# Per-head norm statistics kept in 16 rows, with root and reciprocal there, and spread back by matmuls

## The reference, cut to what matters

```python
# RWKV, before the scan
kk = (k * k_k).reshape(hd)                    # hd = (b, t, 16 heads, 64)
kk = kk / jnp.maximum(jnp.linalg.norm(kk, axis=-1, keepdims=True), 1e-12)
# RWKV, after the scan
mean = jnp.mean(y, axis=-1, keepdims=True)
var = jnp.mean(jnp.square(y - mean), axis=-1, keepdims=True)
y = (y - mean) * lax.rsqrt(var + RW_LNX_EPS) * lnx_w + lnx_b
y = y + jnp.sum(rh * kh * r_k, axis=-1, keepdims=True) * vh
out = (y.reshape(b, t, c) * g) @ w_o
# latent attention, rmsnorm per head
q_nope = rmsnorm(q[..., :64], qn_norm)        # 16 heads of 64
q_pe = rope(rmsnorm(q[..., 64:], qr_norm), pos)   # 16 heads of 32
k_nope = rmsnorm(einsum('...r,rhd->...hd', c, w_uk), kn_norm)
```

## Time and profile before

| | us |
|---|---|
| median of the runs (3) | 3170.84 |
| lowest, highest | 3169.41, 3178.54 |
| span of the profiled execution | 3169.1 |
| PE busy | 2695.0 (85%) |
| DVE busy | 1607.7 (51%) |
| ACT busy | 1070.8 (34%) |
| POOL busy | 174.8 (6%) |

### The profile page before, as it was taken

One profiled execution on the slowest core, in us unless ns is written; L12 is line 12 of the kernel. 1 busy time (PEld: TensorE's weight loads), 2 busy tenths in 40 slices (PEclk: granted clock), 3 DMA queues, 4 the chain that ended last, 5 costly groups with the idle time before them and its releaser, 6 DMA issues. The chain is left out here.

```text
span 3169.1 us, 48791 instructions
## 1 busy us (share of the span) xinstructions
PE 2695.0 (85%) x21151; PEld 2385.4 (75%) x21151; DVE 1607.7 (51%) x2358; ACT 1070.8 (34%) x1798; POOL 174.8 (6%) x176
## 2 busy tenths in 40 slices
PE   6939985998847899979989888978997939985999
PEld 5728854998724678869989866678997718864999
DVE  5384336644362577756434843265536374326643
ACT  4333112433311344434334620044434332203442
POOL 0020011000000000000000132200000020011000
PEclk8969867999865899989999965589998978967999
DMA  4210001444200222214434301323442210001442
GB/s 152 90 66 3 6 28 60 153 147 159 98 0 0 67 67 67 67 54 157 149 124 146 138 27 63 131 99 120 147 147 104 83 40 30 6 27 53 147 151 105
DMA packets 44133, 275.70 MB, mean 87 GB/s; under 512 B 5216, under 2 KB 5248, under 8 KB 14096
## 3 DMA queue, kind: packets, MB, share of 16 engines
q1 hardware_dynamic: 43680, 271.95, 24.1%
q0 software_dynamic: 240, 0.64, 0.1%
HBM read 256.32 MB, written 16.24 MB: 86 GB/s over the span
## 5 line engine op out<-in xcount | busy, mean ns | idle before, releaser
L315 PE MATMUL banks<-rounded,rounded 128*128 128x320 f32 x3184 | 1009.8, 317 | 165.3 <-DVE rounded L331 69.1
L316 PE MATMUL banks<-rounded,rounded 128*128 128x320 f32 x3184 | 995.7, 313 | 0.0
L317 PE MATMUL banks<-rounded,rounded 128*128 128x320 f32 x3184 | 995.2, 313 | 0.0
L305 DVE TENSOR_TENSOR rounded<-weight_ring,rounded 128x1024 fp32r<-128x1024 f32 x398 | 487.2, 1228 | 513.4 <-ACT rounded L298 513.1
L315 PEld LDWEIGHTS banks<-rounded,rounded 128*128 128x128 f32 x3184 | 609.4, 191 | 177.3 <-DVE rounded L331 74.3
L316 PEld LDWEIGHTS banks<-rounded,rounded 128*128 128x128 f32 x3184 | 609.7, 191 | 3.6
L317 PEld LDWEIGHTS banks<-rounded,rounded 128*128 128x128 f32 x3184 | 608.8, 191 | 0.0
L298 ACT ACTIVATE rounded<-weight_ring 128x1024 fp32r<-128x1024 f32 x398 | 419.2, 1058 | 414.6 <-PE banks L317 360.1
L942 PE MATMUL banks<-arena 64*64 64x64 f32 x4032 | 146.3, 225 | 22.8 <-PEq L788 20.3
L942 PEld LDWEIGHTS banks<-arena 64*64 64x64 f32 x4032 | 134.4, 140 | 31.0 <-issue 29.2
L470 ACT ACTIVATE arena<-banks 128x320 f32<-128x320 f32 x128 | 56.0, 438 | 247.9 <-PE banks L317 247.9
(11 more groups left out here) (361 smaller groups left out, 3593.1 us busy)
## 6 DMA issues: line engine op xcount, KB each, us to landing
weight_ring<-in_panels SPq DMA_DIRECT2D x206, 1024.0 KB, 4.7
arena<-in_pages SPq DMA_DIRECT2D x64, 320.0 KB, 3.4
arena<-in_ssm SPq DMA_DIRECT2D x8, 1024.0 KB, 4.8
out_ssm_sample<-arena SPq DMA_DIRECT2D x8, 1024.0 KB, 3.8
arena<-in_wkv SPq DMA_DIRECT2D x2, 2048.0 KB, 8.2
out_wkv_sample<-arena SPq DMA_DIRECT2D x2, 2048.0 KB, 6.2
consts<-in_consts SPq DMA_DIRECT2D x1, 1673.5 KB, 9.7
residual<-in_x SPq DMA_DIRECT2D x1, 1280.0 KB, 5.6
```

The costliest lines, as they stand in the source:

```text
L305: self.k.nc.vector.tensor_tensor(self.k.w_lo[:, i % SPLIT], self.raw(i), self.k.w_hi[:, i % SPLIT].bitcast(F32), ALU.subtract)\
L315: mm(out, hi, x_hi, start=start, stop=False)
L316: mm(out, hi, x_lo, start=False, stop=False)
L317: return mm(out, lo, x_hi, start=False, stop=stop)
```

## The change

Two constants are added, `pick64` and `pick32`, and two helpers. `pick(w, i)` is a window of 16 columns with which a product of a tile's squares puts the means of its heads into their rows of a 16-row result; eight (four) products add up to the statistics of all heads in one bank. `spread` copies rows back: for each head of a tile, one product of a broadcast column of the identity with the 16 rows fills the head's 64 (32) partitions of a bank. Root, clamp and reciprocal then run on 16 rows of 320 (256) columns.

- In the preparation, DVE multiplies the keys straight from the spread banks; PE's bonus products wait for these products (`kk`).
- In the output, DVE scales from the spread banks; bias, gate and remainder follow in an interleaved order on DVE; POOL has no part any more, and the third weight remainder is put in front of the reciprocal.
- In the latent projection, ACT squares rotary queries and keys tile by tile inside the loop; PE sums two tiles later (`stat`), and spreads queries (`to_rows`) within the loop from tile 22 on through three banks in turn; the key rows are spread behind the rotation's products.

```diff
+    for w, n in ((64, 30), (32, 28)):
+        add(f"pick{w}", (np.arange(n)[None] == n - 16 + p[:, None] // w) / w)
+    def pick(self, w, i):
+        c, n = CONST_COLS[f"pick{w}"]
+        first = n - 16 - P // w * i
+        return self.consts[:, c + first:c + first + 16]
+    def spread(self, out, w, i, rows):
+        c, _ = CONST_COLS["ident"]
+        for n in range(P // w):
+            h = P // w * i + n
+            ins = self.nc.tensor.matmul(out[n * w:(n + 1) * w, :], self.consts[0:16, c + h:c + h + 1].to_broadcast([16, w]), rows,
+                                        start=True, stop=True)
+        return ins
...
# preparation, DVE
-            for g in range(2):
-                vec.wait_ge(*pe_did.at("norm", 4 * g + 3))
-                v.tensor_scalar(g3(T2)[:, 4 * g:4 * g + 4, :], allbanks[:, 4 * g:4 * g + 4, :], 1e-24 / 64, None, ALU.max)\
...
-                v.reciprocal(T2[:, h], T2[:, h]).then_inc(*vec_did.tick("inv", g))
+            vec.wait_ge(*pe_did.at("norm"))
+            v.tensor_scalar(inv, k.bank(0, T)[0:16, :], 1e-24 / 64, None, ALU.max).then_inc(*vec_did.tick("clamp"))
+            vec.wait_ge(*act_did.at("root"))
+            v.reciprocal(inv, inv).then_inc(*vec_did.tick("inv"))
             for i in range(KT):
-                ins = v.scalar_tensor_tensor(T1[:, cols(i)], K[:, cols(i)], k.param(f"k_k{j}", i), T2[:, cols(i)], ALU.mult, ALU.mult)
+                vec.wait_ge(*pe_did.at("inv", i))
+                ins = v.scalar_tensor_tensor(T1[:, cols(i)], K[:, cols(i)], k.param(f"k_k{j}", i), k.bank(i, T), ALU.mult, ALU.mult)
# preparation, PE
-                nc.tensor.matmul(k.bank(i, T), k.const("mean64"), T2[:, i * T:(i + 1) * T], start=True, stop=True)\
+                ins = nc.tensor.matmul(k.bank(0, T)[0:16, :], k.pick(64, i), T2[:, i * T:(i + 1) * T], start=i == 0, stop=i == KT - 1)
+            ins.then_inc(*pe_did.tick("norm"))
+            pe.wait_ge(*vec_did.at("inv"))
+            for i in range(KT):
+                k.spread(k.bank(i, T), 64, i, inv).then_inc(*pe_did.tick("inv", i))
+            pe.wait_ge(*vec_did.at("kk"))
...
# output, DVE
+            split.lo(vec, 2)
+            vec.wait_ge(*act_did.at("root"))
+            v.reciprocal(RS, RS).then_inc(*vec_did.tick("rs"))
+            for n in range(KT + 4):
+                if n < KT:
+                    vec.wait_ge(*pe_did.at("rs", n))
+                    v.scalar_tensor_tensor(Y[:, n, :], Y[:, n, :], k.param(f"lnx_w{j}", n), k.bank(n, T), ALU.mult, ALU.mult)\
+                        .then_inc(*vec_did.tick("w", n))
...
+                if 0 <= n - 2 < KT:
+                    i = n - 2
+                    vec.wait_ge(*vec_did.at("b", i))
+                    v.tensor_tensor(Y[:, i, :], Y[:, i, :], G[:, i, :], ALU.mult).then_inc(*vec_did.tick("gated", i))
+                if 0 <= n - 4 < KT:
+                    rest_vec(k, vec, act_did, vec_did, lambda i: Y[:, i, :], yh, yl, n - 3, first=n - 4)
# latent projection, PE, in the loop over tiles n
+                if 9 <= n < 29:
+                    stat(*kinds[n - 2])
+                if 22 <= n < 26:
+                    to_rows("p", n - 22)
+                if 26 <= n < 31:
+                    to_rows("q", n - 26)
+            for i in range(5, KT):
+                to_rows("q", i)
+            pe.wait_ge(*vec_did.at("qpn", 3))
...
+            pe.wait_ge(*vec_did.at("rk"))
+            pe.wait_ge(*vec_did.at("qn", KT - 1))
+            for i in range(KT):
+                ins = k.spread(k.ps[:, 4 + i // 2, (i % 2) * TP:(i % 2 + 1) * TP], 64, i, RK)
# latent projection, ACT, in the loop: roots of 16 rows behind tiles 17, 20 and 28
+                if n == 17:
+                    act.wait_ge(*pe_did.at("stat", "qn"))
+                    s.activation(RQ, k.ps[0:16, 4, 0:T], ACT.Sqrt, bias=k.eps(0, slice(0, 16))).then_inc(*act_did.tick("rootq"))
...
# latent projection, DVE
             v.reciprocal(RQ, RQ).then_inc(*vec_did.tick("rq"))
-            v.scalar_tensor_tensor(QN, QN, gain, RQ, ALU.mult, ALU.mult).then_inc(*vec_did.tick("qn"))
+            for i in range(KT):
+                vec.wait_ge(*pe_did.at("rows", "q", i))
+                v.scalar_tensor_tensor(QN[:, i, :], QN[:, i, :], gain, k.bank((7, 4, 5)[(4 + i) % 3], T), ALU.mult, ALU.mult)\
+                    .then_inc(*vec_did.tick("qn", i))
+                if i == 5:
+                    vec.wait_ge(*act_did.at("rootk"))
+                    v.reciprocal(RK, RK).then_inc(*vec_did.tick("rk"))
```

More of the change, by code:

```diff
@@ L851, in _ @@
             ins.then_inc(*act_did.tick("factor"))
[L852 to L855, removed]
+            act.wait_ge(*vec_did.at("clamp"))
+            s.activation(inv, inv, ACT.Sqrt, scale=64.0).then_inc(*act_did.tick("root"))
             act.wait_ge(*pool_did.at("before"))
@@ L1192, in stage_rwkv_output @@
     flat = lambda a: a.rearrange("p a b -> p (a b)")
[L1193 removed]
+    SQ, RS = k.at(RW["AR"], KT, T), k.at(RW["BK"], T, rows=16)
     yh, yl = k.rounded(RW["BK"] + W, KT, T), k.rounded(RW["BK"] + 2 * W, KT, T)
@@ L1208, in _ @@
                 pe.wait_ge(*act_did.at("sq", i // 4))
-                nc.tensor.matmul(k.bank(i, T), k.const("mean64"), SQ[:, i, :], start=True, stop=True).then_inc(*pe_did.tick("var", i))
-            pe.wait_ge(*act_did.at("root", 1))
+                ins = nc.tensor.matmul(k.bank(0, T)[0:16, :], k.pick(64, i), SQ[:, i, :], start=i == 0, stop=i == KT - 1)
+            ins.then_inc(*pe_did.tick("var"))
+            pe.wait_ge(*vec_did.at("rs"))
+            for i in range(KT):
+                k.spread(k.bank(i, T), 64, i, RS).then_inc(*pe_did.tick("rs", i))
             out_project_pe(k, pe, split, yh, yl, KT, lambda e, i: e.wait_ge(*vec_did.at("xl", i)))
@@ L1219, in _ @@
             split.hi(act, 1)
-            for g, fs in halves:
-                act.wait_ge(*pe_did.at("var", 4 * g + 3))
-                nc.scalar.activation(RS[:, fs, :], allbanks[:, fs, :], ACT.Sqrt, bias=k.eps(1)).then_inc(*act_did.tick("root", g))
+            act.wait_ge(*pe_did.at("var"))
+            nc.scalar.activation(RS, k.bank(0, T)[0:16, :], ACT.Sqrt, bias=k.eps(1, slice(0, 16))).then_inc(*act_did.tick("root"))
             split.hi(act, 2)
-            round_act(k, act, act_did, pool_did, lambda i: Y[:, i, :], yh, KT, "gated")
+            round_act(k, act, act_did, vec_did, lambda i: Y[:, i, :], yh, KT, "gated")
             out_project_act(k, act, split, KT)
[L1227 to L1231, removed]
         @block.vector
@@ L1240, in _ @@
                 split.lo(vec, i)
[L1241 to L1248, removed]
+            split.lo(vec, 2)
[6 more added lines that the diff above has]
+                        .then_inc(*vec_did.tick("w", n))
+                if 0 <= n - 1 < KT:
+                    i = n - 1
                     vec.wait_ge(*vec_did.at("w", i))
```

85 lines of the change are left out of this document (41 added, 44 removed).

## The result

The changed kernel takes 3103.09 us (median of 4 runs, 3097.12 to 3114.55), the one before 3171.61 beside it: ratio 0.978, 95% interval 0.977 to 0.980. That is 68.5 us faster where 53.8 were forecast, and 0.9 us under the low end of the range. The profiled execution took 3105.45 us with a span of 3103.7, 65.4 us less than the span before.

The account below looks back on a forecast made before the run. The prediction took VectorE's reciprocals to bound the three changed stretches. Savings of 2 x 9.1 + 2 x 12.4 + 11.0 - 0.2 = 53.8 us off 3170.8 gave 3117 us, range 3104 to 3140.

Parts of the forecast that it names:

- Preparation: Two preparations: short root and reciprocal, then eight spreads at 1.07 us a bank; 9.1 us saved each.
- Output: Two outputs: short reciprocal, DVE the bound from the fourth bank at 1.83 us a bank; 12.4 us saved each.
- Latent projection: One latent projection: sums and spreads move into the tile loop, shortening the tail behind it; 11.0 us saved.
- Each inserted sum or spread pays two changes: Latent projection's loop: every inserted small matmul pays two changes of matmul shape, 0.2 us each, beside its passes.
- The part behind the loop: Latent projection after its tile loop: few full-sized matmuls there, so rotations and key spreads were priced at 1.2 GHz.
- I take the loop at 2.4 GHz and rotations and key spreads at 1.2 GHz, 5.6 more: Latent projection: lower clock only behind the loop adds 5.6 us, cutting the saving from 16.6 to 11.0 us.
- Rival 1: Clock rises during the spreads and stays up, also through the latent projection: 3107 us, chance 0.17.
- Rival 2: Clock falls in the latent loop with the first spread and stays down to the stage's end: 3138 us, chance 0.25.
- Rival 3: Column blocks of the spreads do not overlap, at 1.2 GHz, making the kernel slower: 3193 us, chance 0.03.

Follow-up runs that it names:

- gate_pool: Changed kernel with the output's gating put back on GpSimd, all else the same: 3100.54 us.
- pairs: Changed kernel with the latent projection's sums placed in pairs behind every second tile: 3098.18 us.
- latent_only: Changed kernel with the preparation and output changes taken back, so only the latent projection is changed: 3154.81 us.
- halves: Changed kernel with the spreads of preparation and output reordered, all upper 64-column matmuls first, then all lower: 3129.08 us.
- pairs_gate_rope: Changed kernel with latent sums paired, output gating on GpSimd, and the sine product ahead of the key products: 3104.61 us.

## Why the prediction was right and where it failed

- **Preparation: right, step by step.** Root, 2.14 us reciprocal at 176.28, pitch 1.07 at 0.50, end 187.87; 9.0 saved of 9.1.
- **Output: right within 1.3 us, in part by luck.** The first output tile was ready 35.0 us after the stage's start at 451.9 (forecast about 35). VectorE is the bound from the fourth tile on, as forecast, and at 1.72 us a tile in place of 1.83 its last remainder came 0.8 us earlier than forecast; but the tile then took 2.1 us more and not 1.1, as TensorE's passes at the lower clock lagged behind. The two misses cancel. gate_pool, meant to take load off VectorE, slowed its biases, and so does not show by itself how far behind TensorE is. In layer 3 the old output was 1.3 us longer than in layer 0, and so the saving there 13.7.
- **Latent projection: the failed step.** "Each inserted sum or spread pays two changes", at 0.2 each. Between the copies of the first and the last tile this made 25.5 us of additions (the 26.4 of the prediction less one spread, which follows the last tile). The loop is 54.4 long against 33.2: 21.1. Seven of the eight spreads there stand directly behind a sum and share a change with it: 0.67 in place of 0.93, while the one alone between tiles cost 0.88. That is 1.9 us. Two changes around a sum cost 0.31 and not 0.4: the twelve sums of 320 columns at 0.84 in place of 0.93 are 1.1, the eight of 256 at 0.74 in place of 0.83 are 0.7. 0.4 is the first tile, which in the kernel before met the lower clock, a piece of luck; 0.2 is a slip in the sum, where 9 x 0.93 was put at 8.6 and is 8.4. Together 4.3 of the 4.4.
- **The part behind the loop, same term: the second failed step.** "I take the loop at 2.4 GHz and rotations and key spreads at 1.2 GHz, 5.6 more". The loop held 1.00. Behind it mainly the rotations met the lower clock (3.81 us; 2.42 in pairs); the key spreads ran at 0.93 on the mean. It took 14.9 us, 869.96 to 884.87, where 18.5 and the ninth spread's 0.9 were forecast: 4.5 less. Without the surcharge that step had 13.8, and pairs and latent_only, whose clock stayed up there, took 13.3 (in pairs 862.05 to 875.32). latent_only has the same instructions in this stage as the changed kernel, so the stage alone does not decide whether the clock falls there; what does was not found. The two parts are the 8.9 us missing.
- **Rivals.** Rival 1's 3107 us is nearer than the forecast, by one half of its mechanism and by luck: the upper clock behind the latent loop mostly came, but the spreads of preparation and output stayed at 0.50, as the earlier trace rows had it, and that the sums were cheaper was in neither. Of the Trainium skill's rule that matmul activity lifts the throttle (TensorE: Matmul & The Clock Gate, section Part 1: The HAM clock gate) the runs show both sides: in the sums, of 128 rows, the clock rose from 0.50 to 1.00, and in 8.5 us of spreads, of 16 rows and back to back, it did not. Rival 2 is refuted: 1.00 throughout the loop's last 28 us. Rival 3 is refuted by 1.07, and halves shows that the order of the heads is what it hangs on.
- **What was not priced.** Unchanged stretches differ between these kernels by up to 7.5 us in a scan and 10.6 in the attention, with either sign; from before to after one scan lost 5.0, the other gained 1.5, the latent front 3.0 and the attention 1.6. The unchanged preparation of layer 0 took 20.5 to 20.9 us in gate_pool, pairs and pairs_gate_rope, where its spreads began at the upper clock before they lost it (7.92 to 8.27 us in place of 8.80). For the latent front one cause is seen: TensorE idles ahead of the latent sums (3.61 us in both), and in the kernel before the clock fell there, in the one after it did not. Windows of PE alone, first of before, then of after:

```profile
816.00:820.00 4.00, 0.51 (x4) 0.84 0.77 262
820.00:825.00 5.00, 4.88 (x9) 0.50 0.00 0
```

```profile
793.00:797.00 4.00, 0.67 (x3) 1.00 0.61 246
797.00:802.00 5.00, 3.36 (x13) 1.00 0.00 0
```

  What decides it in the attention, where the first 100 us run at a mean of 0.50 to 0.64 in all of them, was not tested and stays open.

## What to carry to other kernels

Price small matmuls that are put between large ones by the changes of shape in the finished order, not by the operation: neighbours of one shape share them, and a spread behind a sum cost 0.67 us against 0.88 alone. Here a reciprocal's time went by its columns (2.14 us for 16x320, 2.15 for 128x320, 8.15 for 128x1280), so statistics that repeat over rows are inverted once in few rows and spread back, with neighbouring matmuls in different column groups. A few us won by holding the clock up in one stage are not won until the stages behind it have been timed too.

## What had not been expected of the hardware

- Four 32-column blocks overlap as two 64-column ones do: a bank of either kind cost 0.67 us beside a sum at the upper clock; four blocks of two passes at 0.27 in a row would be 2.1.
- Matmuls of 16 rows did not bring the upper clock, and did not always keep it: 8.5 us of them stayed at 0.50; with fillers in front, 4.52 us held 0.95 in one stage, and in another they lost it within 7.48 us, TensorE being busy throughout.
- VectorE's bias with two SBUF operands took 0.69 to 1.15 us beside GpSimd in place of 0.55; the scaling, with a bank as one operand, stayed at 0.53 to 0.55.
